# The end of a recurrent branch's head normalisation moved from VectorE to GpSimd, and four places where the order of instructions changes

## The chip, the cores and the metric

The kernel runs on one core of a Trainium2 chip. The metric is the device time of one execution in microseconds (us). The times shown are of whole executions; the profile is of one further execution. All matrix products are float32 products that are split in two parts (below), so TensorE (PE) carries most of the work, while VectorE (DVE), ScalarE (ACT) and GpSimd (POOL) prepare its operands.

## What is computed

The reference is two transformer blocks of two layers each, one after the other, on a sequence of 256 tokens with 1024 features. In the first block each layer mixes tokens with four branches side by side (windowed attention, a recurrent branch of the RWKV-7 kind, attention with forget gates, attention on 64 selected keys) and merges them with gates; a feed-forward part follows, dense in layer 0 and with 8 experts in layer 1. The second block has a mixer, a cross-attention to 256 memory tokens and a feed-forward part in each layer; the mixer of its second layer is gated linear attention. What the change touches is this:

```python
def rwkv7_branch(...):                      # first block, both layers
    ...
    ym = jnp.mean(y, axis=-1, keepdims=True)
    yv = jnp.mean(jnp.square(y - ym), axis=-1, keepdims=True)
    y = ((y - ym) * lax.rsqrt(yv + RWKV_GN_EPS)).reshape(B, S, RWKV_W) * gn_g + gn_b
    bonus = (jnp.sum(r_h * k_h * r_k, axis=-1, keepdims=True) * v_h).reshape(B, S, RWKV_W)
    return ((y + bonus) * g).astype(p.dtype)

def mixer_block(...):                       # the merge, first block
    for i, (o, w) in enumerate(zip((o_swa, o_rwkv, o_fox, o_dsa), w_rows)):
        merged = merged + gates[:, :, i] * (o @ w)
    return merged @ w_out

def mem_cross_attention(h, mem_n, ...):     # second block, both layers
    s = jnp.einsum('bqhd,bkhd->bhqk', q, k) * (X_HEAD_DIM ** -0.5)
    p = jax.nn.softmax(s, axis=-1)
    o = jnp.einsum('bhqk,bkhd->bqhd', p, v).reshape(Bn, S, D_MODEL)
    return o @ w_out
```

## The kernel before

**Weights.** Every weight matrix is cut into units of 128x2048 elements, which are numbered through the whole program. The DMA queue of SyncE brings a unit into one of four buffers (`RAW`). ACT copies it to a rounded form (`WH`, "high", two buffers; `split_high`, L1811, called through `ahead(u)`, which splits the unit after `u`), and DVE subtracts that from the raw unit (`WL`, "low", in place of the raw unit; `low(u)`, L2488). PE multiplies the high and the low half of the activations with `WH`, and then the high half with `WL`. A buffer of `WH` comes free when PE has finished the unit that held it.

**Order.** There is no scheduler: each engine has its instructions written out by hand, and waits for counters (semaphores). `step` and `signal` on DVE and ACT make an engine wait for its own last instruction. So an instruction that waits holds up all that stand behind it on its engine.

**Attention of the first block (`attention`, mix stage).** There are 16 units (a pair of heads by 128 queries). In step i, PE makes the scores of unit i (L1024), pieces of the gate projection as filling (L1153 with `WH`, L1157 with `WL`), the context of unit i-2 (L1054) and the transposed probabilities of unit i-1 (L1042). DVE takes the scores of unit i (L2483 and L2547), normalises the probabilities of unit i-1 (L2560 to L2562; PE's L1042 waits for it), and then runs `beside(i)`: a low half of a gate unit, where one is due, and further work. In step 2 that is the end of the head normalisation of the recurrent branch (L2799 to L2806): the reciprocal of the roots in `E[1]`, product, gain and bias, the bonus, and the gate. From step 3 to 10 it is two rounds of key selection (`select`, L2778 and L2779).

**Merge.** For each branch PE multiplies the branch's output by its weights (L821, L824), DVE multiplies the product by the gate (L2846), POOL adds it (L745), and for the last branch DVE adds the first two pieces of it (L2849) and POOL the last two. The sum in four pieces is split for the last product `@ w_out`: high on ACT (`mrg_high`, L2072), low on DVE (`mrg_low`, L2823). PE's `down` (L985) starts when the first low piece is there.

**Cross-attention (`xa`).** There are 8 units of one head by 128 queries, in 11 steps, on all engines. `ot_high` on ACT (L1823) and `ot_low` on DVE (L2510) split the output of a head for the last product, of which PE does the first two units between the steps: `down(u0 + 6)` in front of step 7, `down(u0 + 7)` behind it.

**Linear attention (`gla`).** Twelve units of projections are multiplied in order; ACT computes the logarithm of the decays in between (L2376 to L2380), and DVE goes on from there (L2483, L3337, L3339).

Of the kernel before, what the change touches and what calls it, by code (L numbers as in the profile page):

```python
# [7 lines left out]
S = 256  # L8
# [131 lines left out]
N_GATES = 16  # L140
# [157 lines left out]
def program(nc, a, out):  # L298
# [6 lines left out]
    with ctx:  # L305
# [81 lines left out]
        def col(name, n=0):  # L387
            return COL[:, _AT[name] + n:_AT[name] + n + 1]
# [321 lines left out]
        def _(pool):  # L710
# [16 lines left out]
            for L in range(DEPTH):  # L727
                lora(L)
                if L == 0:
                    pool.dma_start(RW[:, :, :], a["router_w"][0].rearrange("(k p) n -> p k n", p=P))\  # L730
                        .then_inc(sem("small_in"), 16)
                    pool.dma_start(G1[:, :, :], a["od_w_g1_2"][0].rearrange("(k p) n -> p k n", p=P))\
                        .then_inc(sem("small_in"), 16)

                pool.wait_ge(sem("shift_done"), L + 1)
                nc.gpsimd.memset(G[:, 16:24, :], 0.0).then_inc(sem("grams_cleared"), 1)
                pool.wait_ge(sem("rwkv_done"), L + 1)
                rows("mix", L, 0)
                for k in (0, 1, 2, 3, 4, 5, 6, 7, 10, 11):
                    fp = (k % 2 + 2 * (k // 4)) if k < 8 else k - 8  # L740
                    pool.wait_ge(sem("merge_taken"), 16 * L + k + 5)
                    if k > 1:
                        pool.wait_ge(sem("merge_added"), 10 * L + min(k - 1, 8))
                    acc = MRG[:, 2 * fp:2 * fp + 2, :]
                    nc.gpsimd.tensor_tensor(acc, MTMP[:, k % 4, :, :], acc, ALU.add)\  # L745
                        .then_inc(sem("merge_added"), 1)
                if L == 0:
                    pool.wait_ge(sem("normed"), 2)
                    rows("ffn", L, 1)
# [1032 lines left out]
        def _(act):  # L1782
# [150 lines left out]
            def mix(L):  # L1933
# [102 lines left out]
                def beside(i):  # L2036
                    if i == 1:
                        act.wait_ge(sem("gn_var"), L + 1)
                        av(E[1], bank[7][:, :], ACT.Sqrt, scale=1.0 / HD, bias=col("eps_gn")).then_inc(sem("gn_root"), 1)
                    if i == 11:  # L2040
                        ot_high([(0, 4)], n0 + 8)

# [266 lines left out]
            def xa(L):  # L2309
# [35 lines left out]
                for i in range(11):  # L2345
# [3 lines left out]
                        queries_out(3)  # L2349
                    if i in (1, 3):  # L2350
                        values_out(i // 2)
                        ahead(u0 + 5 + i // 2)
                    if 2 <= i < 10:
                        pt_out(n0 + i - 2, units[i - 2])
                    if i >= 3:
                        ctx_out(n0 + i - 3, units[i - 3])
                    if i in (4, 6, 8, 10):
                        p = i // 2 - 2
                        ot_high([PAIRS[p]], n0 + 2 * p + 2)
# [4 lines left out]
            def gla():  # L2364
                u0 = U0["gla"]
                for i in range(4):
# [3 lines left out]
                    if i == 1:  # L2370
                        act.wait_ge(sem("gla_psum"), 1)
                        av(GL1, bank[6][0:16, 0:S], ACT.Copy).then_inc(sem("g1_ready"), 1)

                act.wait_ge(sem("gla_psum"), 2)
                for h in range(4):
                    last = av(GB[:, h * S:(h + 1) * S], half(2 + h // 2)[:, h % 2, :], ACT.Identity, bias=col("b_g", h))  # L2376
# [2 lines left out]
                step(av(GE, GE, ACT.Exp, scale=-1.0))  # L2379
                av(GE, GE, ACT.Ln, bias=1.0).then_inc(sem("gl_ready"), 1)  # L2380
                for i in range(4, 12):
                    ahead(u0 + i)
                    if i < 8:
                        feat_out("gla", i, 2 * (i - 4))
                    else:
# [76 lines left out]
        def _(dve):  # L2462
# [127 lines left out]
            def mix(L):  # L2590
# [193 lines left out]
                def beside(i):  # L2784
# [5 lines left out]
                    if i == 0:  # L2790
# [3 lines left out]
                        signal(v.tensor_tensor(E[0], yt, yt, ALU.mult), "gn_square")  # L2794
                        index_scores(1)
                        step(v.tensor_tensor(SCORE, SCORE, admit, ALU.add))
                    if i == 2:
                        dve.wait_ge(sem("gn_root"), L + 1)
                        step(v.reciprocal(E[1], E[1]))  # L2799
                        step(v.tensor_tensor(yt, yt, E[1], ALU.mult))  # L2800
                        for f in range(2):
                            last = v.tensor_scalar(YT[:, f, :], YT[:, f, :], col(f"gn_g{L}", f), col(f"gn_b{L}", f),
                                                   ALU.mult, ALU.add)
                        step(last)
                        step(v.tensor_tensor(YT, YT, OT[:, 6:8, :], ALU.add))
                        signal(v.tensor_tensor(OT[:, 4:6, :], YT, GG, ALU.mult), "rwkv_done")  # L2806
                    if 3 <= i < 11:
                        select(2 * i - 6)
                        select(2 * i - 5)
# [15 lines left out]

                for _, _, parts in BRANCHES:
                    for c in range(2):
                        if u > gates + N_GATES:
                            low(u + 1)
                        if u == gates + N_GATES + 5:  # L2830
                            mrg_low(0)
                            mrg_low(1)
                        for br, _, _, _ in parts:
                            if c == 0 and 4 * br + 3 >= RAW_GATE:
                                dve.wait_ge(sem("gates_open"), OPENED * (L + 1) - 3 + br)
# [467 lines left out]
            def xa(L, former):  # L3303
# [4 lines left out]
                for i in range(4):  # L3308
# [6 lines left out]
                    signal(ins, "q_scaled")  # L3315
                    low(u0 + 2 + i)
                for i in range(11):
                    if i < 8:
                        scaled(n0 + i, units[i])
                    if 1 <= i < 9:  # L3320
                        normalised(n0 + i - 1, units[i - 1])
                    if i in (2, 4, 8):
                        low(u0 + {2: 6, 4: 7, 8: 8}[i])
                    if i in (5, 7, 9, 10):
                        p = {5: 0, 7: 1, 9: 2, 10: 3}[i]
                        ot_low(stage, p, [PAIRS[p]], dst=OT8L)
                low(u0 + 9)

# [188 lines left out]
```

## Time and profile before

| | |
|---|---|
| time, median of 3 runs (lowest to highest) | 2286.12 us (2285.44 to 2290.88) |
| profiled execution: its own time | 2292.18 us |
| profiled execution: span of its instructions | 2290.4 us |
| mean granted TensorE clock in it | 0.983 of full speed |
| busy: PE, DVE, ACT, POOL | 95%, 67%, 54%, 2% of the span |
| bytes read from memory | 397.76 MB, 174 GB/s over the span |

The profiled execution took 6 us more than the median; 1.8 us of its time lie outside the span. A PE that is busy for 95% of the span leaves some 107 us in which it waits. The waits are short and each stands at a place of its own, so they are read one by one. In the rows, a start time is counted from the start of the span, and a bracket at the end of a row tells how long the engine had been idle before it and whose instruction it waited for.

### The profile page before, as it was taken

What the parts mean: (1) busy time and instruction counts of PE and PEld (TensorE: products, weight loads), DVE (VectorE), ACT (ScalarE), POOL (GpSimd) and SP (SyncE); (2) the same over time, 40 slices, a digit from 0 to 9 for tenths busy, and PEclk for the clock granted to TensorE, in tenths of its full rate; (3) what the DMA queues carried; (4) which work ended last, traced back from release to release, by engine and by line L of the source; (5) the groups of instructions that cost most, each with busy time, mean ns of one, the idle gap of its engine ahead of it and who ended that gap; (6) DMA issues with size and microseconds to landing.
All of it is one profiled execution on the core that took longest, in us unless ns stands there. A gap on an engine that the chain in (4) does not pass through costs nothing.

```text
span 2290.4 us, 36708 instructions
## 1 busy us (share of the span) xinstructions
PE 2183.0 (95%) x14655; PEld 1918.6 (84%) x14655; DVE 1545.2 (67%) x2063; ACT 1244.5 (54%) x1789; POOL 53.4 (2%) x51
## 2 busy tenths in 40 slices
PE   7999989999999988999999998999899999998999
PEld 7988878888988867888888886988788889887887
DVE  4758677747758676676688887876477456565774
ACT  4526646545535644454467776566565355565652
POOL 0000030000000030000000000000000000000000
PEclk9999999999999988999999999999999999999999
DMA  7524357655424329667599996534366543443664
GB/s 244 149 65 129 120 170 193 184 199 150 144 73 131 108 97 245 189 183 200 175 321 337 333 337 213 180 129 150 108 177 190 188 143 129 147 148 108 186 184 146
DMA packets 426632, 400.98 MB, mean 175 GB/s; under 512 B 21056, under 2 KB 392000, under 8 KB 426352
## 3 DMA queue, kind: packets, MB, share of 16 engines
q1 hardware_dynamic: 424192, 391.39, 54.9%
q0 software_dynamic: 2288, 7.48, 1.0%
q8 instruction: 107, 1.75, 0.3%
q14 instruction: 45, 0.37, 0.1%
HBM read 397.76 MB, written 1.05 MB: 174 GB/s over the span
## 4 chain that ended last, share of the span: by engine, by line
PE 82%; DVE 10%; ACT 5%; issue 3%; DMA 1%; SPq 0%; DVEq 0%; ACTq 0%
PE bank L1359 15%; PE bank L985 13%; PE bank L1362 8%; PE bank L821 5%; PE bank L1527 4%; PE bank L1153 4%; PE bank L1441 4%; PE bank L1549 3%; PE bank L824 3%; DVE WL L2488 3%; PE bank L1530 2%; PE bank L1157 2%; PE bank L931 2%; ACT WH L1811 2%; PE bank L913 1%
## 5 line engine op out<-in xcount | busy, mean ns | idle before, releaser
L2488 DVE TENSOR_TENSOR WL<-RAW,WH 128x2048 fp32r<-128x2048 f32 (+1 forms) x290 | 657.4, 2269 | 358.6 <-ACT WH L1811 356.1
L1811 ACT ACTIVATE WH<-RAW 128x2048 fp32r<-128x2048 f32 (+1 forms) x290 | 547.8, 1889 | 167.6 <-PE bank L985 115.2
L1359 PE MATMUL bank<-XTB,WH 128*128 128x512 f32 x1312 | 330.2, 394 | 4.4 <-ACT WH L1811 4.4
L1359 PEld LDWEIGHTS bank<-XTB,WH 128*128 128x128 f32 x1312 | 237.1, 190 | 47.3 <-issue 4.8
L1362 PEld LDWEIGHTS bank<-XTB,WL 128*128 128x128 f32 x1248 | 170.2, 190 | 12.2
L1362 PE MATMUL bank<-XTB,WL 128*128 128x256 f32 x1248 | 174.0, 282 | 0.0
L1153 PE MATMUL bank<-XTB,WH 128*128 128x256 f32 x1024 | 146.0, 293 | 3.5 <-ACT WH L1811 2.2
L1153 PEld LDWEIGHTS bank<-XTB,WH 128*128 128x128 f32 x1024 | 132.1, 196 | 10.9 <-issue 3.7
L2117 ACT ACTIVATE WK<-bank 128x256 f32<-128x256 f32 x132 | 43.4, 381 | 149.5 <-PE bank L1362 135.1
L821 PE MATMUL bank<-XTB,WH 128*128 128x256 f32 x896 | 120.5, 288 | 3.3 <-ACT WH L1811 3.3
L821 PEld LDWEIGHTS bank<-XTB,WH 128*128 128x128 f32 x896 | 113.3, 194 | 6.0 <-ACT WH L1811 3.5
L2488 DVE TENSOR_TENSOR XWL<-XRAW,WH 128x2048 fp32r<-128x2048 f32 (+1 forms) x40 | 89.5, 2238 | 34.9 <-ACT WH L1811 34.6
L1811 ACT ACTIVATE WH<-XRAW 128x2048 fp32r<-128x2048 f32 (+1 forms) x40 | 74.9, 1873 | 16.6 <-PE bank L1441 7.9
L1157 PE MATMUL bank<-XTB,WL 128*128 128x256 f32 x512 | 78.1, 297 | 0.2 <-DVE WL L2488 0.2
L2206 ACT ACTIVATE WK<-bank 128x256 f32<-128x256 f32 x66 | 21.7, 381 | 100.0 <-PE bank L1362 100.0
L1527 PE MATMUL bank<-WH,XTB 128*128 128x512 f32 (+1 forms) x328 | 75.6, 374 | 0.0
L2488 DVE TENSOR_TENSOR WL<-RAW,XWH 128x2048 fp32r<-128x2048 f32 (+1 forms) x26 | 58.5, 2250 | 22.8 <-ACT XWH L1811 22.7
L1157 PEld LDWEIGHTS bank<-XTB,WL 128*128 128x128 f32 x512 | 68.6, 199 | 5.0 <-issue 2.9
L985 PE MATMUL bank<-WL,HIDH 128*128 128x512 f32 x264 | 66.7, 391 | 0.0
L985 PE MATMUL bank<-WH,HIDH 128*128 128x512 f32 x264 | 66.3, 389 | 0.0
L985 PE MATMUL bank<-WH,HIDL 128*128 128x512 f32 x264 | 66.2, 389 | 0.0
L824 PE MATMUL bank<-XTB,WL 128*128 128x256 f32 x448 | 63.5, 284 | 2.8 <-DVE WL L2488 2.8
(549 smaller groups left out, 4043.6 us busy)
## 6 DMA issues: line engine op xcount, KB each, us to landing
RAW<-in_exp_w SPq DMA_DIRECT2D x144, 512.0 KB, 5.4
XRAW<-in_exp_w SPq DMA_DIRECT2D x112, 512.0 KB, 5.3
RAW<-in_w_in SPq DMA_DIRECT2D x106, 512.0 KB, 4.7
RAW<-in_ffn_w_gu SPq DMA_DIRECT2D x88, 512.0 KB, 5.0
RAW<-in_ffn_w SPq DMA_DIRECT2D x66, 512.0 KB, 4.4
RAW<-in_ffn_w_down SPq DMA_DIRECT2D x44, 512.0 KB, 4.1
RAW<-in_xa_w_kv SPq DMA_DIRECT2D x32, 512.0 KB, 4.5
RAW<-in_od_w_in SPq DMA_DIRECT2D x24, 512.0 KB, 4.3
```

The costliest lines, as they stand in the source:

```text
L821: mm(dst, wh[:, k, c:c + P], x[:, k0 + j, :], start=(i == 0 and j == 0), stop=False)
L824: last = mm(dst, wl[:, k, c:c + P], src[0][:, k0 + j, :], start=False, stop=(j == n - 1))
L985: last = mm(bank[2 + 2 * t + h][:, :], x[:, k0 + k, t * P:(t + 1) * P], w[:, k, h * 512:(h + 1) * 512], start=(first and k == 0), stop=(en ...
L1153: mm(dst, whi(u)[:, k, c:c + P], x[:, k, :], start=(x is XT[0] and k == 0), stop=False)
L1157: last = mm(dst, wlo(u)[:, k, c:c + P], XTH[:, k, :], start=False, stop=(k == KT - 1))
L1359: mm(dst[:, :], wh[:, k, e * P:(e + 1) * P], XTB[:, :, k, :], start=(k == 0), stop=False)
L1362: last = mm(dst[:, 0:S], wl[:, k, e * P:(e + 1) * P], XTH[:, k, :], start=False, stop=(k == KT - 1))
L1441: last = mm(bank[2 + 2 * t + h][:, :], x[:, t * P:(t + 1) * P], w[:, k, h * 512:(h + 1) * 512], start=(i == 0 and k == 0 and n == 0), stop ...
L1527: mm(dst, x[:, k0 + k, tokens], whi(u)[:, k, :], start=(k0 + k == 0 and x is XTH), stop=False)
L1549: last = mm(bank[6 + h][:, :], x[:, 2 * i + k, :], w[:, k, h * 512:(h + 1) * 512], start=(i == 0 and k == 0 and n == 0), stop=(i == N_CHUN ...
L1811: av(whi(u), raw(u), ACT.Copy).then_inc(sem("wh_ready"), 1)
L2488: v.tensor_tensor(wlo(u), raw(u), whi(u).bitcast(fp32), ALU.subtract).then_inc(sem("wl_ready"), 1)
```

## The change

The end of the head normalisation leaves DVE's step 2. The reciprocal stays on DVE, in two halves of 256 columns, one in step 3 and one in step 4, and all that follows it (two products, two gains with bias, the bonus, the gate) is issued on POOL. `rwkv_done` now counts eight instructions a layer. ACT waits for the last of them in step 10. Four orders change beside it: in the merge DVE makes the first two low pieces of the sum ahead of the low half of a weight unit; in the cross-attention ACT splits a weight unit after it has copied out the probabilities and the context of the step, and DVE splits the second pair of output tiles at the start of step 7 and not at its end; in the linear attention ACT splits one weight unit ahead of the decays and not after them.

```diff
 # POOL, layer L of the first block
                 nc.gpsimd.memset(G[:, 16:24, :], 0.0).then_inc(sem("grams_cleared"), 1)
-                pool.wait_ge(sem("rwkv_done"), L + 1)
+                for f in range(2):
+                    pool.wait_ge(sem("rwkv_done"), 8 * L + 2)
+                    nc.gpsimd.tensor_tensor(YT[:, f, :], YT[:, f, :], E[1][:, S * f:S * (f + 1)], ALU.mult).then_inc(sem("rwkv_done"), 1)
+                for f in range(2):
+                    pool.wait_ge(sem("rwkv_done"), 8 * L + 4)
+                    nc.gpsimd.tensor_scalar(YT[:, f, :], YT[:, f, :], col(f"gn_g{L}", f), col(f"gn_b{L}", f), ALU.mult, ALU.add)\
+                        .then_inc(sem("rwkv_done"), 1)
+                pool.wait_ge(sem("rwkv_done"), 8 * L + 6)
+                nc.gpsimd.tensor_tensor(YT, YT, OT[:, 6:8, :], ALU.add).then_inc(sem("rwkv_done"), 1)
+                pool.wait_ge(sem("rwkv_done"), 8 * L + 7)
+                nc.gpsimd.tensor_tensor(OT[:, 4:6, :], YT, GG, ALU.mult).then_inc(sem("rwkv_done"), 1)
+                pool.wait_ge(sem("rwkv_done"), 8 * L + 8)
                 rows("mix", L, 0)
 # ACT, beside(i) in the attention of the first block
+                    if i == 10:
+                        act.wait_ge(sem("rwkv_done"), 8 * L + 8)
 # ACT, cross-attention, steps 0 to 10
                     if i in (1, 3):
                         values_out(i // 2)
-                        ahead(u0 + 5 + i // 2)
                     if 2 <= i < 10:
                         pt_out(n0 + i - 2, units[i - 2])
                     if i >= 3:
                         ctx_out(n0 + i - 3, units[i - 3])
+                    if i in (1, 3):
+                        ahead(u0 + 5 + i // 2)
 # ACT, linear attention
+                ahead(u0 + 4)
                 act.wait_ge(sem("gla_psum"), 2)
                 for h in range(4):
                     last = av(GB[:, h * S:(h + 1) * S], half(2 + h // 2)[:, h % 2, :], ACT.Identity, bias=col("b_g", h))
...
                 for i in range(4, 12):
-                    ahead(u0 + i)
+                    if i > 4:
+                        ahead(u0 + i)
 # DVE, beside(i) in the attention of the first block
-                    if i == 2:
+                    if i in (3, 4):
                         dve.wait_ge(sem("gn_root"), L + 1)
-                        step(v.reciprocal(E[1], E[1]))
-                        step(v.tensor_tensor(yt, yt, E[1], ALU.mult))
-                        for f in range(2):
-                            last = v.tensor_scalar(YT[:, f, :], YT[:, f, :], col(f"gn_g{L}", f), col(f"gn_b{L}", f),
-                                                   ALU.mult, ALU.add)
-                        step(last)
-                        step(v.tensor_tensor(YT, YT, OT[:, 6:8, :], ALU.add))
-                        signal(v.tensor_tensor(OT[:, 4:6, :], YT, GG, ALU.mult), "rwkv_done")
+                        part = E[1][:, S * (i - 3):S * (i - 2)]
+                        v.reciprocal(part, part).then_inc(sem("rwkv_done"), 1)
 # DVE, merge
-                        if u > gates + N_GATES:
-                            low(u + 1)
                         if u == gates + N_GATES + 5:
                             mrg_low(0)
                             mrg_low(1)
+                        if u > gates + N_GATES:
+                            low(u + 1)
 # DVE, cross-attention, steps 0 to 10
+                    if i == 7:
+                        ot_low(stage, 1, [PAIRS[1]], dst=OT8L)
...
-                    if i in (5, 7, 9, 10):
-                        p = {5: 0, 7: 1, 9: 2, 10: 3}[i]
+                    if i in (5, 9, 10):
+                        p = {5: 0, 9: 2, 10: 3}[i]
                         ot_low(stage, p, [PAIRS[p]], dst=OT8L)
```

Three places show what stands in a row now. The line numbers of the changed kernel are a little higher; the same operations are L2483 and L2499, L2488 and L2504, L2799 and L2816, L2823 and L2833.

VectorE before, attention of the first block in layer 0, from the normalising of unit 1 in step 2 to the first rounds of key selection in step 3 (`WK` holds the roots and the branch's output, `SMX` the scores):

```order
L2562 TENSOR_TENSOR SMX<-SMX,TINY 128x512
L2488 TENSOR_TENSOR WL<-RAW,WH 128x2048
L2799 RECIPROCAL WK<-WK 128x512
L2800 TENSOR_TENSOR WK<-WK 128x512
L2802 TENSOR_SCALAR WK<-WK,COL 128x256 x2
L2805 TENSOR_TENSOR WK<-WK,OT 128x512
L2806 TENSOR_TENSOR OT<-WK 128x512
L2483 SCALAR_TENSOR_TENSOR SMX<-bank,CST 128x512
L2547 TENSOR_REDUCE TINY<-SMX 128x2
```

VectorE of the change at the same place:

```order
L2578 TENSOR_TENSOR SMX<-SMX,TINY 128x512
L2504 TENSOR_TENSOR WL<-RAW,WH 128x2048
L2499 SCALAR_TENSOR_TENSOR SMX<-bank,CST 128x512
L2563 TENSOR_REDUCE TINY<-SMX 128x2
L2499 SCALAR_TENSOR_TENSOR TINY<-SROW,TINY 128x2
L2576 TENSOR_TENSOR TINY<-TINY 128x2
L2577 RECIPROCAL TINY<-TINY 128x2
L2578 TENSOR_TENSOR SMX<-SMX,TINY 128x2x128
L2504 TENSOR_TENSOR WL<-RAW,WH 128x2048
L2816 RECIPROCAL WK<-WK 128x256
L2794 MAX TINY<-OT 128x8
```

The scores of unit 3 (the row of 128x512) now follow the low half directly, and a half of the reciprocal stands behind the next low half; its twin stands at the same place one step later.

VectorE before, end of the merge (`XTB<-WK,XTB` is a low piece of the sum):

```order
L2846 TENSOR_TENSOR WK<-G,bank 128x512
L2849 TENSOR_TENSOR WK<-WK 128x512
L2488 TENSOR_TENSOR WL<-RAW,WH 128x2048
L2823 TENSOR_TENSOR XTB<-WK,XTB 128x512 x2
L2846 TENSOR_TENSOR WK<-G,bank 128x512 x2
L2488 TENSOR_TENSOR WL<-RAW,WH 128x2048
L2823 TENSOR_TENSOR XTB<-WK,XTB 128x512 x2
```

VectorE of the change, the same place from the low pieces on:

```order
L2833 TENSOR_TENSOR XTB<-WK,XTB 128x512 x2
L2504 TENSOR_TENSOR WL<-RAW,WH 128x2048
L2856 TENSOR_TENSOR WK<-G,bank 128x512 x2
L2504 TENSOR_TENSOR WL<-RAW,WH 128x2048
L2833 TENSOR_TENSOR XTB<-WK,XTB 128x512 x2
```

The first two low pieces and the low half of the weight unit have changed places.

ScalarE before, linear attention, from the output of the fourth projection unit to that of the fifth (`G<-bank` and `F<-bank` are the outputs):

```order
L1869 ACTIVATE G<-bank 128x2x256
L2376 ACTIVATE G<-bank,COL 128x256 x4
L2378 ACTIVATE G<-G 128x1024
L2379 ACT_TABLE_LOAD
L2379 ACTIVATE G<-G 128x1024
L2380 ACT_TABLE_LOAD
L2380 ACTIVATE G<-G 128x1024
L1811 ACTIVATE WH<-RAW 128x2048
L1869 ACTIVATE F<-bank 128x512
```

ScalarE of the change at the same place:

```order
L1880 ACTIVATE G<-bank 128x2x256
L1822 ACTIVATE WH<-RAW 128x2048
L2391 ACTIVATE G<-bank,COL 128x256 x4
L2393 ACTIVATE G<-G 128x1024
L2394 ACT_TABLE_LOAD
L2394 ACTIVATE G<-G 128x1024
L2395 ACT_TABLE_LOAD
L2395 ACTIVATE G<-G 128x1024
L1880 ACTIVATE F<-bank 128x512
```

The high half of the weight unit stands ahead of the decays instead of behind them.

## Rows read from the trace of the kernel before

**Rows 1.** The page's busy times.

```profile
PE 2183.0 (95%) x14655; PEld 1918.6 (84%) x14655; DVE 1545.2 (67%) x2063; ACT 1244.5 (54%) x1789; POOL 53.4 (2%) x51
```

**Rows 2.** PE's waits: waiter and waited-for, us in total, times, longest us.

```profile
PE bank L985 <- DVE XTB L2823: 7.1, 2, 3.6
PE bank L1042 <- DVE SMX L2562: 4.9, 5, 1.8
PE bank L985 <- DVE OT8L L2510: 2.5, 2, 1.2
```

**Rows 3.** Timeline of DVE, attention of layer 0: start, us, engine, line, operation.

```profile
183.01 3.35 DVE L2799 RECIPROCAL WK<-WK 128x512 f32<-128x512 f32 x1
...
188.62 0.69 DVE L2806 TENSOR_TENSOR OT<-WK 128x512 f32<-128x512 f32 x1
189.34 0.69 DVE L2483 SCALAR_TENSOR_TENSOR SMX<-bank,CST 128x512 f32<-128x512 f32 x1
...
204.45 0.43 DVE L2562 TENSOR_TENSOR SMX<-SMX,TINY 128x256 f32<-128x256 f32 x1
```

**Rows 4.** Timeline of PE in the same stretch.

```profile
183.81 0.70 PE L1024 MATMUL bank<-F 64*128 64x256 f32 x4
...
191.86 0.44 PE L1042 MATMUL bank<-CST,SMX 128*128 128x128 f32 x2 [1.77 <-DVE SMX L2562]
...
204.94 0.44 PE L1042 MATMUL bank<-CST,SMX 128*128 128x128 f32 x2 [0.19 <-DVE SMX L2562]
```

**Rows 5.** Windows: PE, PEld, DVE, ACT, POOL busy; PEclk; DMA share; GB/s.

```profile
193.40:196.90 3.50, 3.35 (x16) 3.05 (x16) 3.32 (x9) 2.00 (x2) 0.00 (x0) 0.52 0.68 249
309.40:312.80 3.40, 3.40 (x10) 2.68 (x9) 3.33 (x4) 0.63 (x1) 2.58 (x2) 0.53 0.12 47
1427.60:1429.60 2.00, 0.06 (x1) 0.06 (x1) 0.92 (x2) 0.80 (x3) 2.00 (x4) 1.00 0.51 193
1429.60:1433.00 3.40, 3.11 (x24) 2.85 (x25) 1.51 (x6) 2.18 (x8) 0.89 (x2) 1.00 0.90 277
1627.20:1630.60 3.40, 3.40 (x15) 2.82 (x16) 2.09 (x2) 1.54 (x1) 0.00 (x0) 1.00 0.52 144
```

**Rows 6.** Timeline of DVE and PE, end of the merge of layer 0.

```profile
305.06 1.08 DVE L2849 TENSOR_TENSOR WK<-WK 128x512 f32<-128x512 f32 x1
306.06 2.28 DVE L2488 TENSOR_TENSOR WL<-RAW,WH 128x2048 fp32r<-128x2048 f32 x1
308.26 1.28 DVE L2823 TENSOR_TENSOR XTB<-WK,XTB 128x512 fp32r<-128x512 f32 x2
309.00 5.52 PE L985 MATMUL bank<-WH,XTB 128*128 128x512 f32 x16 [3.56 <-DVE XTB L2823]
```

**Rows 7.** One line of POOL: ns of one min/median/max, first and last start, shape.

```profile
L745 POOL TENSOR_TENSOR WK<-WK x20: 1280/1298/3347, 293.1 to 823.0; 128x512 f32<-128x512 f32 x20
```

**Rows 8.** Timeline of ACT, DVE and PE in the linear attention.

```profile
1873.73 1.57 ACT L2376 ACTIVATE G<-bank,COL 128x256 f32<-128x256 f32 x4 [1.32 <-PE bank L1705]
...
1881.04 1.89 ACT L1811 ACTIVATE WH<-RAW 128x2048 fp32r<-128x2048 f32 x1
...
1882.98 3.67 PE L821 MATMUL bank<-XTB,WH 128*128 128x256 f32 x16 [3.35 <-ACT WH L1811]
...
1885.17 1.22 DVE L2483 SCALAR_TENSOR_TENSOR G<-G 128x1024 f32<-128x1024 f32 x1
...
1889.53 2.29 DVE L2488 TENSOR_TENSOR WL<-RAW,WH 128x2048 fp32r<-128x2048 f32 x1
```

**Rows 9.** Timeline of ACT, DVE and PE, cross-attention, first layer of the second block.

```profile
1612.17 0.41 PE L1081 MATMUL bank<-CST,SMX 128*128 128x128 f32 x2 [0.87 <-ACT PT L1910]
...
1617.03 0.41 PE L1081 MATMUL bank<-CST,SMX 128*128 128x128 f32 x2 [0.60 <-ACT PT L1910]
...
1619.29 0.63 ACT L1823 ACTIVATE OTH<-OT 128x512 fp32r<-128x512 f32 x1
...
1627.13 2.12 PE L985 MATMUL bank<-WH,OTH 128*128 128x512 f32 x8 [1.23 <-DVE OT8L L2510]
```

## The prediction

> **What bounds the kernel.** The page first: PE is busy for 2183.0 of 2290.4 us [rows 1], so at most 107 us can be won without less matrix work, and each edit is worth what it takes out of PE's waits. The list of PE's waits says which of them the edits touch: the first low piece of the merged sum 7.1 us in two waits, the normalised probabilities 4.9 us in five, the second output pair of the cross-attention 2.5 us in two [rows 2]; and one wait of 3.35 us for a high half in the linear attention [rows 8]. Then the timelines around each wait, for who is late and why. Last the windows behind each wait, because a wait can cost more than itself: for some 3.4 us behind the waits of 1.77 and 3.56 us PE ran at the lower of its two levels, 1.2 GHz and not 2.4 (mean granted share 0.52 and 0.53) [rows 4 to 6]. Half of 3.4 us is lost there: a fall costs about 1.7 us. Behind a wait of 1.23 us the share stayed at 1.00, and so it did once behind a PE that had stood for nearly all of 2 us [rows 5, 9]. So between 1.2 and 2 us of standing a fall is possible and not certain.
>
> **Merge, both layers.** DVE ends its second sum at 305.06 + 1.08 = 306.14, makes a low half of 2.28 us, and then the low pieces; PE starts at 309.00 [rows 6]. The changed order puts the pieces first. The high copy that the first of them needs follows DVE's sum before this one, a step of some 1.7 us, and a copy of 128x512 takes ACT 0.63 us [rows 9], so it is there. The wait shrinks by the low half that no longer stands ahead, 309.00 - 308.26 = 0.74 us behind the start of the pieces: PE starts at 306.14 + 0.74 = 306.88, which is 2.1 us earlier, and the wait is 3.56 - 2.1 = 1.4 us. What is late next: the low half of the first unit, now behind both pieces, ends at 306.14 + 1.28 + 2.28 = 309.7. PE needs it after 16 matmuls with the high half; at the lower clock these take 5.5 us, at the full one an estimate of 5.52 - 1.7 = 3.8, so 310.7 at the earliest. It is hidden with 1 us to spare. The rest of the merge (two products by gates on DVE, two sums on POOL) starts 0.3 us later, while PE gets ahead by 2 to 4 us; I charge 0.2 us for splits that PE reaches a little early. The gain is 2.1 - 0.2 = 1.9 us a layer, and 1.7 more if a wait of 1.4 us does not lower the clock. 1.4 is nearer to 1.23, behind which nothing fell, than to 1.77, so I take the full 3.6 us: **7.2 us for two layers**, with 3.8 as the other end.
>
> **Linear attention.** The high half that PE waits for stands behind the logarithms of the decays on ACT, which run from 1873.73 to about 1881.1 (where the split starts). Ahead of them ACT had stood idle for 1.32 us, and the split takes 1.89 [rows 8]; put there it costs the decays 0.5 us and PE's wait is gone: 3.35 us, and 1.7 of clock, since PE's 16 matmuls behind it took 3.67 us. What is late next: DVE's chain on the decays, at whose end stands the next low half (1889.53, until 1891.82). It started at 1885.17, behind the late low half; now it starts when the decays are there, at 1881.1 + 0.6, so 3.4 us earlier [rows 8], while PE comes 3.35 + 1.7 = 5.1 us earlier. The difference of 1.7 us is the most that PE can wait there, nothing the least; it had waited for nothing there before, so some of it is covered, and I take 1.0. Gain: 5.1 - 1.0 = **4.1 us** (3.4 to 5.1).
>
> **Cross-attention, both layers.** The second pair is high at 1619.29 + 0.63 = 1619.9, and PE wants its low half at 1627.13 - 1.23 = 1625.9 [rows 9]. DVE used to make it only behind the scores of the last unit; made ahead of them it lies in an idle stretch. The wait goes in full: 1.2 us a layer, **2.4 us**, and no clock with it. The new place of ACT's split takes away the wait of 0.87 us for the probabilities of unit 2, but the next wait of this kind, 0.60 us at 1617.03, hangs on DVE's maxima of the unit before, for which nothing changes [rows 9]: PE arrives earlier and waits longer. I count nothing, between 0 and 1.7 us of gain in two layers.
>
> **Attention of the first block, both layers.** Here the edit that gives the change its name does less than it seems. It takes 189.34 - 183.01 = 6.3 us from DVE in front of the scores of unit 3 [rows 3], and puts back two halves of the reciprocal, 3.35 / 2 = 1.7 us each. The scores of unit 3 leave PE at 183.81 + 0.70 = 184.5 [rows 4], so DVE, instead of working, waits from 183.0 to 184.6; it starts 4.7 us earlier. The probabilities of unit 2 are then normalised at about 187.1, and PE's wait of 1.77 us with its clock is gone: PE is 3.5 us ahead. But from here DVE is the engine that has no slack: between 189.34 and 204.88 it works without a pause, and PE already waits again at 204.94, for 0.19 us [rows 3, 4]. The end of that stretch moves by -4.7 + 2 x 1.7 = -1.3 us, to 203.6, while PE would be there 3.5 + 0.2 us earlier, at 201.2. So PE waits about 2.4 us at unit 4 in place of 1.77 at unit 2.
>
> To this comes POOL. It starts when the second half of the reciprocal is done, near 199.4, and its six instructions are near 5.8 us by the only row for it (1.3 us for 512 columns, half for 256, and I give `tensor_scalar` the same) [rows 7]. On top of DVE's own work they are not free: beside POOL a sum of two operands in memory takes DVE 1.08 us [rows 6], the like of it without POOL 0.69 [rows 3], and the longest of POOL's own took 3.35 where the shortest took 1.28 [rows 7]. Between 199.4 and the normalising of unit 4 stand three DVE instructions with two operands in memory (two on a few numbers and the product of the probabilities). Each can lose from nothing to a whole POOL instruction of 1.3 us; I take 0.8 us for all. What is on the path is then 204.4, 0.5 us ahead of before, behind a wait of 3.2 us, and behind such a wait the clock fell each time in the rows (1.77, 3.35, 3.56): 1.7 us. Sum: 1.2 us lost a layer, **2.4 us lost**; without a fall 0.5 us won a layer. After unit 4, steps without a low half give DVE air, and the rest of POOL's chain lies beside it. ACT's new wait in step 10 comes some 40 us after POOL is done: nothing. The two loads behind it on POOL's queue (the norm's rows) start some 15 us later and are used 120 us later: nothing.
>
> The Trainium skill, "SBUF — State Buffer", section "SBUF: two separate sides", says that a GpSimd instruction and a VectorE one with two memory inputs exclude each other for their whole length. By that rule, each of the three that meets POOL waits for its end, and the sum would be up to 1.3 us a layer worse. The trace agrees in kind: 3.35 is about 1.28 and a low half of 2.3 in between, less what overlaps.
>
> **Sum.** -7.2 - 4.1 - 2.4 + 2.4 = -11.3 us. Falls of the clock elsewhere may come and go by chance of their place, 1.7 us each, either way. The profiled 2292.2 would be 2280.9; it stands 6.1 us above the median of the runs, from which the same sum gives 2286.1 - 11.3 = **2274.8 us**.
>
> **Rivals.** (1) The wait of 1.4 us in the merge still lowers the clock in both layers: 3.4 us less is won, 2278.2. For it speaks the fall behind 1.77. (2) DVE and PE meet at unit 4 without a fall of the clock, as once after 2 us of standing: 3.4 us more, 2271.4. (3) POOL excludes DVE more often than I charge, in the first and the second step after it starts: 2.5 us more a layer, 2279.8. (4) On the other side, slower: POOL's instructions with per-partition operands, for which there is no row, are several times longer, and DVE, which has no slack, is shut out for all of them. It decides when each layer loses 11.3 / 2 = 5.7 us more than I charge; at 7.5 us a layer the time is 2290. Against it: POOL's 20 sums took 1.3 us in the median. (5) The change does not do what it says: PE's gains in one place are waits for weights in the next, since the loads follow PE; all but 2 us would be lost, 2284. Against it: in PE's list of waits there is none for a load behind the first one.
>
> **Chances.** Forecast 0.48, (1) 0.20, (2) 0.12, (3) 0.12, (4) 0.04, (5) 0.04. Range: from 2268, which is (2) less one more fall and the full gain in the cross-attention (1.7 us each), to 2281.5, which holds (3), and (1) with half of (3) on top (2280.7). 0.3% is 6.9 us, about what can be told from no change: faster means below 2279.3. The forecast, (1), (2) and about a third of (3) lie there, 0.84; within 0.3% lie the rest of (3), (5) and a part of (4), 0.13; slower 0.03.
>
> **What the profile should show.** No wait of PE at unit 2 in the attention, and one of 2 to 3.5 us at unit 4, in both layers, with a stretch of clock near 0.5 behind it; POOL's six instructions there, 5 to 8 us in all. In the merge a wait of 1.4 us with full clock behind it. In the linear attention no wait for the fifth unit, one near 1 us in the next. In the cross-attention no wait for the second pair, and one near 1.5 us where 0.60 stands. The forecast is wrong if the wait at unit 4 is far from 3 us, or if the clock behaves otherwise at these three places.

## The result, and the profile after

| | before | after |
|---|---|---|
| median of 11 runs each (lowest to highest) | 2290.88 us (2285.42 to 2294.81) | 2281.32 us (2279.76 to 2283.86) |
| profiled execution: its own time, span | 2292.18, 2290.4 us | 2280.61, 2278.8 us |
| mean granted clock in it | 0.983 | 0.984 |

The ratio is 0.9963 with a 95% interval of 0.9953 to 0.9973: 8.5 us faster (6.2 to 10.8). The forecast was 2274.8, or 11.3 us faster. From profile to profile the change is 2280.61 - 2292.18 = -11.6 us. The medians themselves differ by 2290.88 - 2281.32 = 9.6 us, which also lies within the interval. So the change came out smaller in the timed runs than in the one pair of traces, and the level was off by more than that: the forecast is 6.5 us too low, of which 4.8 us are the base (2290.88 measured, 2286.12 taken; four of the 11 runs of before lie at or below 2286.12) and 1.7 us are the change between the medians (9.6 and not 11.3). The measured 2281.32 is 0.2 us below the upper end of the range that I gave, 2281.5.

The page of the kernel after, its busy times [rows 1]:

```profile
PE 2178.7 (96%) x14655; PEld 1915.4 (84%) x14655; DVE 1542.7 (68%) x2055; ACT 1243.4 (55%) x1789; POOL 63.7 (3%) x63
```

Its list of PE's waits (waiter and waited-for, us in total, times, longest), against [rows 2]. No wait for a low half made by `ot_low` is left; a wait of 1.1 us for `OT8L` at another line (L3421) stood in the kernel before too (L3409). Of the three waits in the first row, one of 0.6 us lies in the second block, as it did before.

```profile
PE bank L1053 <- DVE SMX L2578: 8.1, 3, 3.7
...
PE bank L835 <- DVE WL L2504: 3.4, 4, 1.2
...
PE bank L1092 <- ACT PT L1921: 3.0, 4, 1.2
PE bank L996 <- DVE XTB L2833: 2.7, 2, 1.4
```

The merge's waits fell from 7.1 to 2.7 us. The attention's grew from 4.9 to 8.1: the change lost there. The timeline of DVE in the attention of layer 0, against [rows 3]:

```profile
184.16 0.69 DVE L2499 SCALAR_TENSOR_TENSOR SMX<-bank,CST 128x512 f32<-128x512 f32 x1 [1.48 <-PE bank L1035]
...
188.95 1.75 DVE L2816 RECIPROCAL WK<-WK 128x256 f32<-128x256 f32 x1
...
193.44 0.16 DVE L2499 SCALAR_TENSOR_TENSOR TINY<-SROW,TINY 128x2 f32<-128x2 f32 x1
...
196.97 1.75 DVE L2816 RECIPROCAL WK<-WK 128x256 f32<-128x256 f32 x1
...
201.99 0.80 DVE L2499 SCALAR_TENSOR_TENSOR TINY<-SROW,TINY 128x2 f32<-128x2 f32 x1
202.82 0.16 DVE L2576 TENSOR_TENSOR TINY<-TINY 128x2 f32<-128x2 f32 x1
...
203.22 1.18 DVE L2578 TENSOR_TENSOR SMX<-SMX,TINY 128x256 f32<-128x256 f32 x1
```

and of POOL and PE beside it, against [rows 4]:

```profile
198.80 1.43 POOL L739 TENSOR_TENSOR WK<-WK 128x256 f32<-128x256 f32 x2 [145.47 <-DVE WK L2816]
200.34 1.09 POOL L742 TENSOR_SCALAR WK<-WK,COL 128x256 f32<-128x256 f32 x2
201.51 1.26 POOL L745 TENSOR_TENSOR WK<-WK,OT 128x512 f32<-128x512 f32 x1
202.85 1.26 POOL L747 TENSOR_TENSOR OT<-WK 128x512 f32<-128x512 f32 x1
```

```profile
189.62 0.44 PE L1053 MATMUL bank<-CST,SMX 128*128 128x128 f32 x2
194.80 0.66 PE L1053 MATMUL bank<-CST,SMX 128*128 128x128 f32 x4
204.45 0.69 PE L1053 MATMUL bank<-CST,SMX 128*128 128x128 f32 x2 [3.74 <-DVE SMX L2578]
```

PE's wait at unit 2 is gone and one of 3.74 us stands at unit 4. Two of DVE's instructions there take 0.80 and 1.18 us. A step earlier the first took 0.16, and the second is 0.43 in [rows 3]. Their ends follow POOL's: the first ends at 202.79, when POOL's bonus ends at 202.77; the second at 204.40, 0.29 behind the end of POOL's gate at 204.11. That is 0.64 + 0.76 = 1.4 us lost on the path. In layer 1 the same two instructions take 0.79 and 1.18 us, and the wait is 3.73 us at 713.30. The windows of after, behind the wait in layer 0, behind that in layer 1, and behind the two waits of the merge (columns as in [rows 5]; the clock is the sixth figure, without a bracket):

```profile
203.40:206.80 3.40, 2.35 (x10) 1.80 (x11) 3.23 (x8) 2.67 (x10) 1.89 (x3) 0.50 0.29 111
206.80:210.10 3.30, 3.30 (x18) 3.30 (x17) 3.09 (x7) 2.42 (x7) 0.00 (x0) 0.50 0.56 206
210.10:213.50 3.40, 3.40 (x30) 3.10 (x29) 2.56 (x7) 0.28 (x1) 0.00 (x0) 0.98 0.43 109
308.80:312.20 3.40, 3.40 (x15) 2.83 (x16) 3.36 (x3) 1.81 (x2) 0.00 (x0) 1.00 0.80 306
817.50:820.90 3.40, 3.36 (x15) 2.78 (x16) 3.33 (x3) 1.85 (x2) 0.00 (x0) 1.00 0.84 327
711.90:715.30 3.40, 2.00 (x9) 1.45 (x10) 3.19 (x9) 2.67 (x11) 2.21 (x3) 0.52 0.19 59
715.30:718.60 3.30, 3.30 (x17) 3.30 (x17) 3.09 (x7) 2.77 (x7) 0.00 (x0) 0.50 0.74 259
```

The clock stayed low for two such stretches, 6.7 us, where the forecast had one. The first of them begins about a microsecond before PE starts again. The merge, the linear attention and the cross-attention of after, against [rows 6], [rows 8] and [rows 9]:

```profile
308.06 1.47 DVE L2833 TENSOR_TENSOR XTB<-WK,XTB 128x512 fp32r<-128x512 f32 x2
308.80 1.43 PE L996 MATMUL bank<-WH,XTB 128*128 128x512 f32 x5 [1.36 <-DVE XTB L2833]
```

```profile
1879.91 2.29 DVE L2504 TENSOR_TENSOR WL<-RAW,WH 128x2048 fp32r<-128x2048 f32 x1
1882.26 1.22 PE L835 MATMUL bank<-XTB,WL 128*128 128x256 f32 x8 [0.92 <-DVE WL L2504]
```

```profile
1613.16 0.41 PE L1092 MATMUL bank<-CST,SMX 128*128 128x128 f32 x2 [1.19 <-ACT PT L1921]
```

The wait of 1.36 us has the full clock behind it. The linear attention waits 0.92 us for the next low half. The cross-attention keeps one wait of 1.19 us for the probabilities where it had 0.87 and 0.60.

Because both kernels issue the same 14,655 matmuls in the same order, the start of the n-th of after can be set against that of before. Its change over one place ("locally" below) says what was won or lost there: 3.8 us won in each merge, 4.5 in the linear attention, 1.5 in each cross-attention, and 2.4 and 2.3 lost in the two attentions, up to their first ten units. That is 15.1 - 4.7 = 10.4 us; the rest of the 11.6 is mostly falls of the clock at other places.

### The profile page after: what moved, and what is told of

Same layout as the page of the kernel before. It is cut to its first block, busy times and chain, and to the rows that moved or that the text cites. A ratio compares the mean times of both kernels' runs of the same rounds, so it can differ in the third digit from the quotient of the medians.

```text
span 2278.8 us, 36716 instructions
## 1 busy us (share of the span) xinstructions
PE 2178.7 (96%) x14655; PEld 1915.4 (84%) x14655; DVE 1542.7 (68%) x2055; ACT 1243.4 (55%) x1789; POOL 63.7 (3%) x63
## 3 DMA queue, kind: packets, MB, share of 16 engines
q8 instruction: 107, 1.75, 0.3%
HBM read 397.76 MB, written 1.05 MB: 175 GB/s over the span
## 4 chain that ended last, share of the span: by engine, by line
PE 82%; DVE 9%; ACT 5%; issue 3%; DMA 1%; POOL 0%; SPq 0%; DVEq 0%; ACTq 0%; POOLq 0%
PE bank L1370 15%; PE bank L996 12%; PE bank L1373 8%; PE bank L832 5%; PE bank L1164 4%; PE bank L1538 4%; PE bank L1452 4%; PE bank L1560 3%; PE bank L835 3%; DVE WL L2504 2%; PE bank L1168 2%; PE bank L1541 2%; PE bank L942 2%; ACT WH L1822 2%; PE bank L924 1%
## 5 line engine op out<-in xcount | busy, mean ns | idle before, releaser
L2504 DVE TENSOR_TENSOR WL<-RAW,WH 128x2048 fp32r<-128x2048 f32 (+1 forms) x290 | 657.5, 2269 | 344.1 <-ACT WH L1822 341.4
L1164 PEld LDWEIGHTS bank<-XTB,WH 128*128 128x128 f32 x1024 | 132.8, 197 | 10.9 <-issue 3.8
L2504 DVE TENSOR_TENSOR XWL<-XRAW,WH 128x2048 fp32r<-128x2048 f32 (+1 forms) x40 | 89.5, 2237 | 35.0 <-ACT WH L1822 34.7
L2504 DVE TENSOR_TENSOR WL<-RAW,XWH 128x2048 fp32r<-128x2048 f32 (+1 forms) x26 | 58.5, 2250 | 22.8 <-ACT XWH L1822 22.6
```

Of the source, the lines that this page charges most:

```text
L1164: mm(dst, whi(u)[:, k, c:c + P], x[:, k, :], start=(x is XT[0] and k == 0), stop=False)
L2504: v.tensor_tensor(wlo(u), raw(u), whi(u).bitcast(fp32), ALU.subtract).then_inc(sem("wl_ready"), 1)
```

## Experiments

The first four make one part of the change each; they share 29 runs of before (median 2291.57 us, 2284.68 to 2294.16). The other four share 9 runs of it (2290.42, 2285.75 to 2294.86). A gain or a loss against before is (1 - ratio) times that median. Where a run is set against the changed kernel, the figure is the difference of the two medians, which come from different sessions; by the ratios it is 4.8, 6.2, 11.9 and 12.8 us for experiments 5 to 8, up to 1 us from the figures given.

**1. The merge order alone.**

```diff
-                        if u > gates + N_GATES:
-                            low(u + 1)
                         if u == gates + N_GATES + 5:
                             mrg_low(0)
                             mrg_low(1)
+                        if u > gates + N_GATES:
+                            low(u + 1)
```

> The kernel before with the merge order alone. My reading (each order is worth the wait that it takes from PE, and the clock's fall behind it): PE's wait for the first low piece is about 1.4 us in both layers instead of 3.56, the granted clock behind it stays at 1.00, and the time falls by 3.8 us a layer, 7.6 us in all (ratio near 0.9967). If a wait of 1.4 us still lowered the clock when PE arrives at the old time, 4.2 us in all. Rival (gains turn into waits for weights or into falls of the clock elsewhere): less than 4 us.

Measured: 2283.66 us, ratio 0.9968 (0.9956 to 0.9979), 7.3 us won. Locally 3.8 in each layer. The two waits, from the list of PE's waits of this kernel:

```profile
PE bank L985 <- DVE XTB L2823: 2.7, 2, 1.4
```

No clock fell behind either. As forecast, and it is the largest part of the gain.

**2. The order in the linear attention alone.**

```diff
+                ahead(u0 + 4)
                 act.wait_ge(sem("gla_psum"), 2)
...
                 for i in range(4, 12):
-                    ahead(u0 + i)
+                    if i > 4:
+                        ahead(u0 + i)
```

> The kernel before with the order in the linear attention alone. My reading: no wait for the fifth unit, a wait of about 0.9 us at the next low half, 4.7 us won in the profile (ratio near 0.9980). Rival (the decays are late instead): the wait at the next low half is 2 us or more, at most 3 us won.

Measured: 2286.94 us, ratio 0.9988 (0.9979 to 0.9997), 2.7 us won (0.7 to 4.8). Locally 4.5, with this wait at the next low half:

```profile
1886.96 1.22 PE L824 MATMUL bank<-XTB,WL 128*128 128x256 f32 x8 [0.92 <-DVE WL L2490]
```

The mechanism is as read; the runs give less than the trace, at the edge of the interval. The cause of the difference is not shown. One thing in the record bears on it: of the 11 runs, five have a mean granted clock of 0.982 and took 2287.9 to 2289.1 us, and the other six, with 0.984 to 0.987, took 2284.2 to 2286.9; the profiled one (2284.9) is among the six. The median depends on how many fall on either side. The runs of experiment 3 lie apart in the same way (five of 11 at 0.982, 2289.4 to 2290.9; six at 0.985, 2284.9 to 2287.1).

**3. Both orders of the cross-attention alone.**

```diff
 # ACT
                     if i in (1, 3):
                         values_out(i // 2)
-                        ahead(u0 + 5 + i // 2)
...
+                    if i in (1, 3):
+                        ahead(u0 + 5 + i // 2)
 # DVE
+                    if i == 7:
+                        ot_low(stage, 1, [PAIRS[1]], dst=OT8L)
...
-                    if i in (5, 7, 9, 10):
-                        p = {5: 0, 7: 1, 9: 2, 10: 3}[i]
+                    if i in (5, 9, 10):
+                        p = {5: 0, 9: 2, 10: 3}[i]
```

> The kernel before with both orders of the cross-attention alone. My reading: no wait at the second output pair; in each layer one wait of about 1.2 us for the transposed probabilities in place of two of 0.87 and 0.60; 2.4 to 2.8 us won in both layers (ratio near 0.9989). Rival (ACT's new place of the split is itself a gain): over 3.5 us. Rival (it is absorbed): under 1 us.

Measured: 2287.09 us, ratio 0.9989 (0.9980 to 0.9998), 2.5 us won. Locally 1.5 in each layer. From the timeline of PE: the wait for the probabilities that is left, 1.20 us, and the second output pair without one.

```profile
1613.64 0.41 PE L1081 MATMUL bank<-CST,SMX 128*128 128x128 f32 x2 [1.20 <-ACT PT L1910]
...
1622.25 2.09 PE L985 MATMUL bank<-WH,OTH 128*128 128x512 f32 x8
```

The wait for the pair, 1.23 us, is the larger part of the 1.5; the other 0.3 is 0.87 + 0.60 against 1.20. The two orders were never run apart, so which of them gave the 0.3 is argued and not shown.

**4. The move alone,** as in the diff of the change, none of the orders.

```diff
-                    if i == 2:
+                    if i in (3, 4):
                         dve.wait_ge(sem("gn_root"), L + 1)
...
+                        v.reciprocal(part, part).then_inc(sem("rwkv_done"), 1)
```

> The kernel before with the head normalisation's end moved to GpSimd and its reciprocal in two halves, and none of the four orders. My reading: no wait at unit 2, one of about 3.7 us at unit 4 in both layers with the clock low for up to 6.7 us behind it; 3.3 us slower than before in all (ratio near 1.0014, 2 to 5 us slower). Rival (the move helps, and its loss in the trace of the whole change is an accident of the clock): 0 to 3 us faster.

Measured: 2294.26 us, ratio 1.0015 (1.0006 to 1.0024): 3.4 us slower (1.4 to 5.5). Locally 2.4 lost in layer 0 and 1.4 in layer 1, where the clock was low for 3.4 us only. The timeline of PE has the same wait:

```profile
205.66 0.69 PE L1053 MATMUL bank<-CST,SMX 128*128 128x128 f32 x2 [3.74 <-DVE SMX L2575]
```

So the edit that names the change makes the kernel slower, and the rival that called the loss an accident of the clock falls. The four parts sum to -7.3 - 2.7 - 2.5 + 3.4 = -9.1 us, and the whole gave -8.5; each part is known to 1 or 2 us, so that they meet so closely is partly luck.

**5. The four orders without the move.** Experiments 1 to 3 in one kernel; the edit is shown against the changed kernel.

```diff
+                    if i == 2:
+                        step(v.reciprocal(E[1], E[1]))
+                        step(v.tensor_tensor(yt, yt, E[1], ALU.mult))
...
-                    if i in (3, 4):
-                        part = E[1][:, S * (i - 3):S * (i - 2)]
-                        v.reciprocal(part, part).then_inc(sem("rwkv_done"), 1)
```

> The changed kernel without the move: the four orders, and the whole head normalisation on VectorE in step 2 as before. My reading (the parts add up): the local gains of the three single edits in their traces, 7.2 + 4.8 + 2.9 us, are all there, so about 14.9 us faster than before in the profile; against the changed kernel 3 to 4 us faster (ratio to before 0.993 to 0.995). Rival (the move's loss is made good later anyway): the same time as the changed kernel within 1 us.

Measured: 2276.35 us (2275.45 to 2277.90), ratio 0.9942 (0.9928 to 0.9957), 13.3 us faster than before (14.9 forecast) and 5.0 below the median of the changed kernel. The parts add up, and the rival that the loss is made good later falls. In layer 0 the clock stayed up behind the same wait for unit 2. It won nothing: PE came earlier and waited for the next units instead, and at unit 4 it was as late as before, to 0.1 us. From the timeline and the windows of PE:

```profile
192.62 0.44 PE L1042 MATMUL bank<-CST,SMX 128*128 128x128 f32 x2 [1.76 <-DVE SMX L2565]
...
199.02 0.66 PE L1042 MATMUL bank<-CST,SMX 128*128 128x128 f32 x4 [0.58 <-DVE SMX L2565]
...
205.69 0.44 PE L1042 MATMUL bank<-CST,SMX 128*128 128x128 f32 x2 [0.77 <-DVE SMX L2565]
```

```profile
191.80:195.20 3.40, 2.26 (x16) 1.77 (x17) 3.30 (x5) 3.40 (x11) 0.00 (x0) 1.00 1.06 358
699.90:703.30 3.40, 3.30 (x17) 3.00 (x16) 3.23 (x9) 2.07 (x2) 0.00 (x0) 0.52 0.75 270
```

**6. The changed kernel with GpSimd's chain held back to step 9.**

```diff
+                pool.wait_ge(sem("probs_ready"), UNITS[f"mix{L}"][0] + 9)
                 for f in range(2):
                     pool.wait_ge(sem("rwkv_done"), 8 * L + 2)
```

> The changed kernel, with GpSimd's chain held until the probabilities of unit 8 are normalised (step 9, where VectorE stands idle for 3.4 us). The reciprocals stay in steps 3 and 4. My reading (GpSimd's chain costs 1.4 us a layer on the path, VectorE's lack of slack the rest): the two instructions of 0.80 and 1.18 us at unit 4 are back at 0.16 and 0.42, PE's wait at unit 4 is 2.3 us instead of 3.74, and each layer gets 1.4 us back, 2.8 us in all, 1.7 more for each layer in which the clock is low for 3.4 and not 6.7 us behind it. Rival (GpSimd's exclusion is all of the loss): the wait at unit 4 falls below 1 us. Rival (GpSimd has nothing to do with it): the wait stays at 3.7.

Measured: 2275.48 us (2274.63 to 2276.09), ratio 0.9936 (0.9922 to 0.9950), 5.8 us below the changed kernel. The timeline of DVE and PE in layer 0, and the windows behind the wait in layer 0 and in layer 1:

```profile
202.52 0.16 DVE L2500 SCALAR_TENSOR_TENSOR TINY<-SROW,TINY 128x2 f32<-128x2 f32 x1
...
203.11 0.42 DVE L2579 TENSOR_TENSOR SMX<-SMX,TINY 128x256 f32<-128x256 f32 x1
...
203.59 0.44 PE L1054 MATMUL bank<-CST,SMX 128*128 128x128 f32 x2 [2.34 <-DVE SMX L2579]
```

```profile
204.40:207.80 3.40, 3.40 (x18) 3.40 (x17) 3.09 (x11) 3.40 (x9) 0.00 (x0) 0.51 0.00 0
207.80:211.20 3.40, 3.40 (x31) 3.10 (x30) 3.33 (x5) 0.46 (x3) 0.00 (x0) 1.00 0.29 57
709.60:713.00 3.40, 3.40 (x16) 2.85 (x17) 3.09 (x12) 3.40 (x8) 0.00 (x0) 0.52 0.00 0
713.00:716.40 3.40, 3.40 (x31) 3.40 (x30) 3.33 (x5) 1.20 (x7) 0.00 (x0) 1.00 0.14 16
```

The events are as read: 0.16 and 0.42 again, a wait of 2.34 and not 3.74, and the clock low for one stretch and not two. The price that I had given the second stretch, 1.7 us, was too high, because about 1 us of it had passed before PE started. From the start of unit 4's matmuls to the 28th behind it the changed kernel takes 6.0 us in layer 0, this one 5.0 and before 3.5: the clock costs 2.5 us there and 1.5 here. So the gain is 1.4 + 1.0 us a layer, locally 4.7 in all, where 5.8 were measured. A wait of 2.34 us is left, so the exclusion is not the whole wait. But the kernel is now level with experiment 5 (2275.48 and 2276.35), and locally both attentions, up to their first ten units, take what they took before (to 0.1 us): GpSimd's chain beside VectorE, with the low clock behind the longer wait, was all that the move lost, and without it the move wins nothing either. The wait of 2.34 us at unit 4 has taken the place of the one of 1.77 at unit 2.

**7. The halves of the reciprocal in steps 5 and 8.**

```diff
-                    if i in (3, 4):
+                    if i in (5, 8):
                         dve.wait_ge(sem("gn_root"), L + 1)
-                        part = E[1][:, S * (i - 3):S * (i - 2)]
+                        part = E[1][:, S * (i // 8):S * (i // 8 + 1)]
```

> The changed kernel, with the halves of the reciprocal in steps 5 and 8, where VectorE stands idle for 1.7 and 1.2 us behind its work, instead of 3 and 4; the chain stays on GpSimd and now starts near 228 us. My reading (the steps chosen are the fault: VectorE has no slack from step 3 to 5): no wait of PE at unit 2 nor above 0.3 us at unit 4, the scores of unit 4 1.7 us earlier; 6 us a layer over the changed kernel at the most (2.45 lost and 3.7 not won there), 8 to 11 us in both, a time near 2271 to 2273. Rival (PE meets VectorE at a later unit instead): waits of 2 us or more at units 6 to 9, under 4 us won.

Measured: 2270.47 us (2268.14 to 2270.53), ratio 0.9911 (0.9896 to 0.9926), 20 us faster than before and 10.9 below the changed kernel, a little below the 2271 to 2273 that I had read. Locally each attention now wins 3.9 us over before, where the changed kernel loses 2.4. Against experiment 6 only the steps of the reciprocal and the start of the chain differ: 5.0 us (7.8 locally; falls of the clock at other places take some of it back). The chain began at 223.04 and not at 228, beside work of VectorE: its product of the probabilities at 226.43 took 0.89 us and not 0.43, but PE did not wait. No wait at units 2 to 4 in the timeline of PE; in the whole list of PE's waits one of 0.6 us is left for the normalised probabilities, in the second block, where it was before:

```profile
190.10 0.44 PE L1053 MATMUL bank<-CST,SMX 128*128 128x128 f32 x2
195.28 0.66 PE L1053 MATMUL bank<-CST,SMX 128*128 128x128 f32 x4
201.12 0.44 PE L1053 MATMUL bank<-CST,SMX 128*128 128x128 f32 x2
```

**8. The same places, all of it on VectorE.**

```diff
 # against experiment 7; POOL's six instructions and its waits for them go
-                        v.reciprocal(part, part).then_inc(sem("rwkv_done"), 1)
+                        step(v.reciprocal(part, part))
+                    if i == 9:
+                        step(v.tensor_tensor(yt, yt, E[1], ALU.mult))
...
+                        signal(v.tensor_tensor(OT[:, 4:6, :], YT, GG, ALU.mult), "rwkv_done")
```

> As the run before, but with the whole end of the head normalisation on VectorE: halves of the reciprocal in steps 5 and 8, the products, gains, bonus and gate (3 us) in step 9, where VectorE stands idle for 3.4 us. My reading (the place decides, not the engine): within 2 us of the kernel that keeps the chain on GpSimd. Rival (the chain must be on GpSimd for the gain): 3 us or more slower than that one, with a PE wait at units 9 to 11.

Measured: 2268.62 us (2267.43 to 2269.55), ratio 0.9907 (0.9892 to 0.9921), 21 us faster than before and the best of all. Locally 3.8 us won in each attention. VectorE does in step 9 what GpSimd did, in 2.9 us where it had stood idle:

```profile
227.10 0.69 DVE L2807 TENSOR_TENSOR WK<-WK 128x512 f32<-128x512 f32 x1
227.83 0.74 DVE L2809 TENSOR_SCALAR WK<-WK,COL 128x256 f32<-128x256 f32 x2
228.60 0.69 DVE L2812 TENSOR_TENSOR WK<-WK,OT 128x512 f32<-128x512 f32 x1
229.33 0.69 DVE L2813 TENSOR_TENSOR OT<-WK 128x512 f32<-128x512 f32 x1
```

Within 2 us of experiment 7 (1.9, with ranges that overlap): the place decides, not the engine. GpSimd was not needed at all.

## Why the prediction was off

**The step that failed first is the base, "from which the same sum gives 2286.1 - 11.3".** It is 4.8 of the 6.5 us by which the time was missed. I took the sum in the trace, which gave 2280.9 for an execution of 2292.2, and carried it to a median 6.1 us lower. That median stood on three runs and not on enough of them: over 11 runs, these three among them, it is 2290.88, and over the 29 runs of the first four experiments 2291.57. Times near 2286 are not rare (four of the 11, two of the 29 below 2287); that two of three fell there was chance. What differs between them shows in the granted clock: of the 29 runs, the 12 with a mean of 0.985 or more took 2284.7 to 2291.4 us, the 17 with 0.984 or less 2290.8 to 2294.2. Had I used the profiled time alone, 2280.9 would stand against the 2281.32 measured, but partly by luck: a base 1.3 us too high would have hidden a gain forecast 1.7 us too large.

**The sum itself, -11.3, was 1.7 us too hopeful by the medians and 2.8 by the ratio (8.5, 6.2 to 10.8), and its term for the attention was half of what it measured.** By terms:

| | forecast | locally in the trace of after | part alone, timed |
|---|---|---|---|
| merge | -7.2 | -7.6 | -7.3 |
| linear attention | -4.1 | -4.5 | -2.7 |
| cross-attention | -2.4 | -3.0 | -2.5 |
| attention | +2.4 | +4.7 | +3.4 (5.0 between experiment 5 and the changed kernel) |

The merge and the cross-attention came out by their mechanism and size: 1.4 us of wait with full clock, and the wait for the second pair gone in full. In the linear attention the wait of 0.92 us at the next low half is the 1.0 that I took. Its gain has the forecast size in both traces and comes out 1.4 us smaller in the runs; the interval of 0.7 to 4.8 us holds both, so it stays open whether anything is lost there. In the trace the attention is the only term that came out worse than forecast, by 2.3 us; the other three made 1.4 of that good.

In the attention every event was where I put it: scores of unit 3 right behind PE's, no wait at unit 2, the meeting at unit 4, POOL's six instructions in 5.0 us (5.8 forecast). Two sizes were wrong, and by the prediction's own sign (a wait of 2 to 3.5 us at unit 4, one stretch of low clock) both showed. The first is "Each can lose from nothing to a whole POOL instruction of 1.3 us; I take 0.8 us for all": it was 1.4. The second is one fall of 1.7 us behind the wait: the wait had grown to 3.74 us, the clock was low for 6.7 us, and 2.5 us were lost. That is 0.6 + 0.8 us more than charged, near the 1.2 us by which the layer's loss of 2.4 exceeds the forecast 1.2. Experiment 6 shows that the two are one cause: without the exclusion the wait is 2.34 us and the low clock costs 1.5.

On the Trainium skill: "SBUF — State Buffer", section "SBUF: two separate sides", says that a VectorE instruction with two inputs in SBUF and a GpSimd one that reads SBUF exclude each other for the length of an instruction. I set 0.8 us against the up to 0.8 + 1.3 = 2.1 that I had worked out by that rule for three instructions. The trace agrees with the rule in kind: DVE's short instruction took 0.80 us and ended with POOL's at 202.79, the product ended 0.29 us behind POOL's at 204.40, and a third one, as POOL changed from one instruction to the next at 202.8, took its usual 0.16 us. The size, 1.4 us, lies in the middle between my discount and that full 2.1: two of the three met POOL and lost 0.64 and 0.76, less than a whole instruction of 1.26, and the third lost nothing.

Of the rivals, (3), GpSimd excluding VectorE for longer, comes nearest: locally 2.3 us in both layers beyond the 2.4 charged, about half its price of 2.5 a layer, and more than half of that is the clock and not the exclusion. (1), (2) and (4) did not occur: the clock held behind 1.36 us and fell at unit 4, and POOL's instructions with per-partition operands took 0.55 us each. (5) is excluded by experiments 1 to 3. What I had not seen is that the meeting at unit 4 need not exist. I followed the move to the steps it names and priced it there, and did not ask in which steps VectorE stands idle.

## What to carry to other kernels

Work taken off a waited-for engine is worth what its new place costs: here the changed kernel and experiment 7, with the same instructions on the same engines, are 10.9 us apart, and experiments 5 and 8, with all of them on VectorE in step 2 or in steps 5, 8 and 9, 7.7 us; the second engine gave nothing. Before moving work to GpSimd, list the idle stretches of VectorE; if it must go there, hold it back until VectorE is idle, because a one-line wait won 5.8 us. And where the profiled execution lies outside the few runs shown, their median is as doubtful as it is: carry the sum from both, and let the range hold both.

## What was new about the hardware

- Whether the clock falls, and for how long, is not given by the length of a wait alone. Behind PE's wait of 1.76 us for unit 2 the clock fell in 8 of 10 cases (two layers of five kernels), behind the merge's 3.56 us in 7 of 8, behind 1.36 us in none of 12 (two layers of six kernels). The 3.74 us of the changed kernel brought 6.7 us of low clock in both layers, and in experiment 4 in layer 0 and 3.4 us in layer 1. Two waits of 1.05 us with 1.1 us of work between them (two places in each of ten kernels) had low clock from about the second on in 6 of 20 cases.
- GpSimd took 0.73 us for a product of 128x256 elements, 0.55 for gain and bias with per-partition operands, and 1.26 for 128x512; VectorE took 0.69 for the last and 1.75 us for a reciprocal of 128x256.
- Ten traces of almost the same program differ by up to 1.9 us in the wait for the first load of the input (6.5 to 8.4). Part of it is made good at once: set matmul for matmul, the ten lie within 1.3 us of each other at 20 us, and still do at 170.
